# The results of an S5 recurrence leave by ACT's DMA queue instead of GpSimd's

## The reference, cut to what matters

```python
def s5_mixer(u, A_re, A_im, log_dt, B_re, B_im, C_re, C_im, D):
    ...
    lam_bar = jnp.exp(lam * dt)
    b_bar = ((lam_bar - 1.0) / lam)[..., None] * b_cplx
    ...
    def step(h_prev, u_c):
        bu = jnp.einsum('lbgh,gph->lbgp', u_c, b_bar)
        _, h = lax.associative_scan(_linear_recurrence, (a_elems, bu), axis=0)
        h = h + lam_pow[:, None] * h_prev[None]
        y = jnp.real(jnp.einsum('lbgp,ghp->lbgh', h, c_cplx))
        return h[-1], y
    ...
    return y + D.astype(jnp.float32) * uf

# in first_block, for the S5 layer
proj = h @ s5_w_in[j]
branch, gate = jnp.split(proj, 2, axis=-1)
y = s5_mixer(branch, ...)
y = jax.nn.gelu(y)
y = y * jax.nn.sigmoid(y @ s5_w_glu[j] + s5_b_glu[j])
out = (y * jax.nn.silu(gate)) @ s5_w_out[j]
```

## Time and profile before

| what | value |
|---|---|
| median of 3 runs | 4606.95 us (4603.45 to 4607.03) |
| the profiled execution, its own time | 4610.55 us |
| its span, first to last instruction | 4608.8 us |
| granted TensorE clock, mean | 0.945 |
| PE busy | 4185.0 us, 91% |
| PEld, DVE, ACT, POOL busy | 47%, 30%, 19%, 5% |
| scan phase, from the first set's Pm copy to the last Silu | 191.12 to 437.71 us |
| one set, copy L765 to copy L765 | 30.74 to 31.03 us |

### The profile page before, as it was taken

The page is one execution under the profiler, slowest core; times in us unless marked ns, Lnnn a source line. Parts: engine busy times, 40 slices in busy tenths (PEclk is TensorE's granted clock), DMA queues, the critical chain, the costliest instruction groups (busy, mean ns, idle before and its releaser), DMA issues. The chain is left out here.

```text
span 4608.8 us, 32069 instructions
## 1 busy us (share of the span) xinstructions
PE 4185.0 (91%) x13567; PEld 2145.3 (47%) x13567; DVE 1366.2 (30%) x1968; ACT 875.9 (19%) x969; POOL 250.9 (5%) x368
## 2 busy tenths in 40 slices
PE   5897999999798999878999999999899999788887
PEld 2454344444444776443344444444345555454453
DVE  6474113021333542232200000001345542412433
ACT  2111102100243221342200000000233421300122
POOL 0233000000000321120000000000000000000000
PEclk8998999999799999998999999999999999889888
DMA  3223110211001110200111111110101001012001
GB/s 110 72 59 77 43 37 23 64 32 37 15 28 42 28 33 19 64 28 14 38 40 37 37 41 37 32 39 29 42 23 29 26 7 44 7 42 71 7 10 39
DMA packets 287979, 172.91 MB, mean 38 GB/s; under 512 B 24047, under 2 KB 278878, under 8 KB 287582
## 3 DMA queue, kind: packets, MB, share of 16 engines
q1 hardware_dynamic: 248848, 124.86, 9.7%
q0 software_dynamic: 9856, 23.87, 1.9%
q10 hardware_dynamic: 29134, 22.14, 1.7%
HBM read 157.63 MB, written 13.21 MB: 37 GB/s over the span
## 5 line engine op out<-in xcount | busy, mean ns | idle before, releaser
L160 PE MATMUL products<-normed,weights 128*128 128x512 f32 x2176 | 955.8, 600 | 46.0 <-ACT normed L879 36.3
L160 PE MATMUL products<-residual,weights 128*128 128x512 f32 x1696 | 736.3, 595 | 7.1 <-ACT residual L351 6.2
L160 PEld LDWEIGHTS products<-normed,weights 128*128 128x128 f32 x2176 | 416.9, 192 | 570.8 <-issue 562.3
L160 PE MATMUL products<-gate,weights 128*128 128x512 f32 x1408 | 615.0, 597 | 18.8 <-POOLq L3392 7.6
L160 PEld LDWEIGHTS products<-residual,weights 128*128 128x128 f32 x1696 | 323.5, 191 | 414.0 <-issue 409.4
L160 PEld LDWEIGHTS products<-gate,weights 128*128 128x128 f32 x1408 | 269.4, 192 | 361.7 <-issue 338.4
L2402 PE MATMUL products<-normed,weights 128*128 128x512 f32 (+1 forms) x672 | 305.1, 603 | 5.0 <-DVE normed L278 5.0
L2402 PEld LDWEIGHTS products<-normed,weights 128*128 128x128 f32 (+1 forms) x672 | 122.6, 189 | 151.5 <-issue 149.3
L178 PE MATMUL products<-weights,normed 128*128 128x512 f32 x384 | 167.5, 598 | 5.0 <-DVE normed L278 5.0
L3187 POOL DMA_DIRECT2D out_dram<-work x8 | 4.3, 539 | 2488.5 <-ACT work L3176 2483.4
L916 DVE TENSOR_TENSOR residual<-products,residual 128x1024 f32<-128x1024 f32 x32 | 39.2, 1225 | 285.6 <-PE products L160 285.6
(11 more groups left out here) (466 smaller groups left out, 4306.9 us busy)
## 6 DMA issues: line engine op xcount, KB each, us to landing
weights<-in_w_in_dram SPq DMA_DIRECT2D x80, 512.0 KB, 3.8
weights<-in_w_up_dram SPq DMA_DIRECT2D x32, 512.0 KB, 4.1
weights<-in_w_down_dram SPq DMA_DIRECT2D x32, 512.0 KB, 3.9
weights<-in_sgu_w_in_dram SPq DMA_DIRECT2D x24, 512.0 KB, 3.9
weights<-in_s_w_in_dram SPq DMA_DIRECT2D x16, 512.0 KB, 4.1
weights<-in_w_out_dram SPq DMA_DIRECT2D x24, 256.0 KB, 2.8
work<-in_x_dram ACTq DMA_DIRECT2D x8, 512.0 KB, 10.2
branch_scratch<-work POOLq DMA_DIRECT2D x8, 512.0 KB, 2.9
```

The lines of the kernel that those rows point to most:

```text
L160: last = pe.matmul(out[0:cols, half * BANK:(half + 1) * BANK], slot(c, b, kt, cols)[:, k, :], acts[n][:, half * BANK:(half + 1) * BANK], s ...
```

## The change

The eight stores of a set leave POOL's program and stand in ACT's, behind the copy L765 and ahead of the Silu. ACT first waits for its own copy to be complete. The final wait for all stores moves from POOL to ACT as well. The transfers themselves, their shapes and their number stay.

```diff
--- before.py
+++ after.py
@@ -695,12 +695,6 @@
                 n = (S5_T - s_) * S5_H
                 pool.dma_start(within[s_ * S5_H:(s_ + 1) * S5_H, :, s_ * S5_H:S5_T * S5_H],
                                kk_dram[:, i * GC:(i + 1) * GC, 0:n]).then_inc(c.s5_within_loaded, 16)
-
-            pool.wait_ge(c.s5_y_read, i + 1)
-            for s_ in range(S5_T):
-                pool.dma_start(y_out[i * GC:(i + 1) * GC, :, s_, :].rearrange("g h n -> h g n"),
-                               Y[s_ * S5_H:(s_ + 1) * S5_H, :, :]).then_inc(c.s5_y_stored, 16)
-        pool.wait_ge(c.s5_y_stored, 16 * S5_T * S5_C)
 
     def tensor(pe):
         for i in range(S5_C):
@@ -764,7 +758,12 @@
                 act.wait_ge(c.s5_y_stored, 16 * S5_T * i)
             act.activation(Y.rearrange("p (j e) n -> p e j n", e=2), c.pb[:, 2:4, :].rearrange("p e (j n) -> p e j n", j=JC), ACT.Copy)\
                .then_inc(c.s5_y_read, 1)
+            act.wait_ge(c.s5_y_read, i + 1)
+            for s_ in range(S5_T):
+                act.dma_start(y_out[i * GC:(i + 1) * GC, :, s_, :].rearrange("g h n -> h g n"),
+                              Y[s_ * S5_H:(s_ + 1) * S5_H, :, :]).then_inc(c.s5_y_stored, 16)
             act.activation(c.C[:, i, :], take_group(c, act, g0 + i), ACT.Silu).then_inc(c.group_read[(g0 + i) % 2], 1)
+        act.wait_ge(c.s5_y_stored, 16 * S5_T * S5_C)
 
     def vector(dve):
         ch = c.dve_chain
```

## The result

The changed kernel takes 4619.05 us (median of 5 runs, 4617.92 to 4626.58) beside 4603.45 us for the kernel before, run beside it; the ratio is 1.0036, with a 95% interval of 1.0022 to 1.0051. It is slower by 0.2 to 0.5%. The profiled execution took 4617.92 us, its span is 4616.2 us.

The account below looks back on a forecast made before the run. PE, busy 91%, bounds the kernel and waits on ACT's copies at each turn. Queue and end give +3.4 us, the clock +6.0: +9.4, carried to the median 4606.95 as 4616.4 us; range 4600 to 4629.

Parts of the forecast that it names:

- The path: At a turn between sets, each ACT copy is on the chain to PE; ACT has 2.81 us held only by PE.
- D: Length of the eight store issues in ACT's stream per set; taken as 4.26 us, bounds 2.78 to 5.06.
- The turns: KK's copy on ACT starts 1.61 us later in turns 2 to 7, 9.7 us in all; 2.7 in turn 1.
- The formula: Turns lose 6 × (D - 2.65) + (D - 1.54) us; with the end's gain, 8 D - 30.7.
- The clock: Half clock behind PE's longer wait for KK's copy costs 1.7 us per fall; half of seven turns, 6.0 us.
- The end: After the last output copy, POOL's store wait and drain are hidden; ACT's loads start 9.0 us sooner.
- Rival D: At the phase's end POOL's drain isn't hidden, so 9.0 us are missing: +18 us, 4625; chance 0.06.
- The sum: Whole kernel: 3.4 us from queue and end plus 6.0 from the clock, 9.4 us slower, 4616.4.
- rival B: Store issues on ACT are short, so the kernel gets faster, 4598; turning point 3.84 without clock loss; chance 0.22.

## Why the prediction was right, and where its sizes were off

**The path.** That the chain at a turn runs through ACT's copies and that the change takes its slack is shown by the rows of after (no wait ahead of either copy) and by the kernels with four issues, with the Silu moved and with the stores behind KK's copy. PE's wait before the product for X, forecast near 2.7 us, was 2.05 to 2.12 in three turns, 3.33 in the first and 3.63 to 4.69 in three. In those last three the transposes ran at full clock, so that PE came earlier to the same wait.

**D, the eight issues.** Taken as 4.26 us, measured 3.80 (0.31 for the first, about 0.46 for each next). The row of x's loads was the right neighbour, that with eight rows per partition was not. By the Trainium skill's page "DMA: Bandwidth & Descriptors" (Issuing engines are not separate DMA queues) the sequencer's time to start a transfer is usually small beside the transfer. For a single store this trace agrees, with 0.46 us beside 2.5 us from issue to landing. The prediction set the sum of eight issues against one landing and called it a disagreement; what the runs show is that the eight landings overlap while the eight issues add up in ACT's stream, to 3.8 us.

**The turns.** The formula gives 9.2 us with D = 3.80 (12.4 with the D I took). KK's copies began 10.2 us later in all: 2.22 in the first turn (2.7 forecast), 0.95 to 1.1 in turns 2 to 4, 2.22 in the fifth, where one issue took 1.56 us, 1.29 and 1.44 in the last two. A long issue in one of the sets was not in the forecast.

**The clock.** This is the term that was mis-sized: half of seven turns, 6.0 us. It fell in all seven turns, and again in all seven of the second run; 21.7 - 10.2 = 11.5 us, 1.6 per turn, the upper end. Two rows of before, one with and one without a fall, did not make a chance of one half. And the place itself had a row that the prediction didn't use: in all seven turns before, the clock fell to 0.50 for 3.4 us behind the 1.2 us wait ahead of the transposes, as in this window of the turn from set 1 to set 2:

```profile
252.00:255.40 3.40, 3.40 (x26) 2.62 (x27) 0.00 (x0) 1.65 (x2) 3.40 (x7) 0.50 0.45 77
```

So waits far shorter than 2.7 us were followed by a fall here. With PE's wait for KK's copy filled, the clock stayed up at the product for X and the loss behind it was gone, with the stores and ACT's work unchanged: that this fall hangs on PE's idle time is shown. The length of the wait alone doesn't decide, though: in the kernel with the late Silu two waits of 2.8 and 2.9 us had no fall behind them, while 2.04 us in the second run of the changed kernel had. And with only the second wait filled the clock also stayed up at the transposes in five of seven turns, though the 1.2 us wait ahead of them was as before. What else it takes stays open. The Trainium skill's page "Perfetto Trace Analysis" (Matmul Optimizations) says that matmuls should run back to back; the two kernels with filled waits agree, with clocks of 1.00 where it was 0.50, and these two waits of the late Silu do not.

**The end.** Forecast 9.0 us, measured 9.7: the last store was issued at c + 3.28 instead of c + 3.78, and landed 2.1 us later instead of 2.3. Rival D, that the drain isn't hidden, is out.

**The sum.** Forecast +9.4 us, 4616.4; in the phase +12.0, and 4619.05 by the median, inside the range. Between the medians of the one comparison it was +15.6, and +12.4 in the second. That 4619.05 lies only 2.7 us from 4616.4 is in part luck, since the kernel before had 4603.45 in this comparison and not the 4606.95 to which the sum was added. D was 0.46 us smaller than taken, worth 3.7 us by the formula, and the clock 5.5 us larger; the two hid each other in part. D of 3.80 even lies just on the side of rival B (short issues), whose turning point without a clock loss was 3.84: without the clock the change would have come out about even. What decided against B is the clock.

## What to carry to other kernels

A DMA issue is an instruction of the engine that makes it. Count it at its length, 0.3 to 0.5 us in these rows, and put it where that engine waits for another one; behind the next set's last copy the same eight cost nothing. Where a phase ends in a drain, let the engine that has started many transfers finish early and give the last ones to another. When a change lengthens PE's waits, price the clock behind them as well, and where a wait can't be removed, try one product in it whose result is overwritten and that is shorter than the wait; three per wait gave back more than they won here.

## What I had not expected of the hardware

- POOL's drain takes 0.71 us behind 8 transfers, but 9.0 behind 200, at a time when all of them have landed.
- Now and then one issue on ACT's queue takes 1.2 to 1.8 us instead of 0.45: one of the 64 in the first profile of the changed kernel, two in the second. Why stays open.
- The kernel before already loses some 1.5 us in each turn to a half clock behind the 1.2 us wait ahead of L714: 30.7 to 31.0 us, against 29.3 to 29.4 without it.
